# The first S5 output one projection unit later, and the squares of two norms added up on GpSimd

## What is computed

```
proj = h @ w_in + b_in
u_s5, cq, ckv, k_pe, u_sgu, v_sgu, gate_logits = split(proj)

# S5: a diagonal complex state-space model, 32 groups of 16 channels and 64 states
h_re, h_im = scan(a, bu)                 # along the tokens
y = h_re @ c_re - h_im @ c_im + d * u    # then gelu and a gate

# MLA: the two low-rank parts are normed before they are projected up
def rms_norm(x, g):
    return x * rsqrt(mean(x * x) + 1e-6) * g
q  = rms_norm(cq, q_norm)  @ w_q_up      # cq has 384 columns
kv = rms_norm(ckv, kv_norm) @ w_kv_up    # ckv has 256 columns
```

## Time and profile before

| what | value |
|---|---|
| median of three runs | 2423.53 us |
| profiled execution | 2425.12 us |
| its span on the core | 2423.30 us |
| TensorE busy | 2374.9 us, 98% |
| VectorE busy | 1390.1 us, 57% |
| GpSimd busy | 1673.5 us, 69% |
| ScalarE busy | 499.8 us, 21% |
| mean granted TensorE clock | 0.991 |

### The profile page before, as it was taken

How to read it: one execution, slowest core, us unless ns; L and a number is a source line. 1 busy time by engine, 2 the same in 40 slices (tenths; PEclk the granted TensorE clock), 3 DMA queues, 4 the chain that set the end, 5 groups by cost and what they waited for, 6 DMA issues and landing times.

```text
span 2423.3 us, 33639 instructions
## 1 busy us (share of the span) xinstructions
PE 2374.9 (98%) x11893; PEld 1952.5 (81%) x11893; DVE 1390.1 (57%) x1808; ACT 499.8 (21%) x957; POOL 1673.5 (69%) x757
## 2 busy tenths in 40 slices
PE   7999999999999999999999999999999999999998
PEld 5787777878888887888888878888878778888886
DVE  7987333475373477544555465534588577553547
ACT  5434221013000004211112230000132462000000
POOL 5435655777777777666666667777777557777775
PEclk8999999999999999999999999999999999999999
DMA  7222344322322322222222223322323112232331
GB/s 276 68 70 92 130 181 183 109 95 71 109 90 95 111 81 83 84 83 87 91 82 89 85 72 97 114 82 95 110 85 96 56 42 79 96 115 77 100 109 59
DMA packets 61729, 237.87 MB, mean 98 GB/s; under 512 B 7152, under 2 KB 12280, under 8 KB 58048
## 3 DMA queue, kind: packets, MB, share of 16 engines
q1 hardware_dynamic: 55152, 232.09, 28.4%
q10 hardware_dynamic: 6480, 4.51, 0.7%
HBM read 232.37 MB, written 2.10 MB: 97 GB/s over the span
## 4 chain that ended last, share of the span: by engine, by line
PE 85%; DVE 7%; DVEq 2%; ACT 1%; POOL 1%; DMA 1%; POOLq 1%; issue 1%; ACTq 1%
PE gg L696 19%; PE gg L697 19%; PE gg L698 19%; PE babcd L751 3%; PE babcd L752 3%; PE babcd L753 3%; PE gg L1124 2%; PE gg L1125 2%; PE gg L1126 2%; PE babcd L696 1%; PE babcd L698 1%; PE babcd L697 1%; DVE h_lo L2237 1%; DVE tb L2227 1%; DVEq L2228 1%
## 5 line engine op out<-in xcount | busy, mean ns | idle before, releaser
L696 PE MATMUL gg<-h_hi,w_hi 128*128 128x512 f32 x1512 | 595.9, 394 | 0.0
L698 PE MATMUL gg<-h_hi,w_lo 128*128 128x512 f32 x1512 | 589.7, 390 | 0.0
L697 PE MATMUL gg<-h_lo,w_hi 128*128 128x512 f32 x1512 | 589.6, 390 | 0.0
L516 POOL TENSOR_TENSOR w_hi<-raw,zero 128x1024 fp32r<-128x1024 f32 x192 | 378.0, 1969 | 295.9 <-PE gg L698 194.9
L518 POOL TENSOR_TENSOR w_lo<-raw,w_hi 128x1024 fp32r<-128x1024 f32 x192 | 479.8, 2499 | 28.0 <-issue 1.3
L507 POOL TENSOR_TENSOR w_hi<-raw,zero 128x1024 fp32r<-128x1024 f32 (+3 forms) x115 | 260.8, 2267 | 191.6 <-PE babcd L698 82.2
L509 POOL TENSOR_TENSOR w_lo<-raw,w_hi 128x1024 fp32r<-128x1024 f32 (+3 forms) x115 | 339.4, 2951 | 16.4
L696 PEld LDWEIGHTS gg<-h_hi,w_hi 128*128 128x128 f32 x1512 | 284.7, 188 | 63.5 <-issue 3.0
L698 PEld LDWEIGHTS gg<-h_hi,w_lo 128*128 128x128 f32 x1512 | 284.4, 188 | 59.8
L697 PEld LDWEIGHTS gg<-h_lo,w_hi 128*128 128x128 f32 x1512 | 284.5, 188 | 58.8 <-issue 0.3
L2328 DVE TENSOR_TENSOR ta<-ff_s,gg 128x512 f32<-128x512 f32 x63 | 43.3, 687 | 313.8 <-PE gg L698 313.8
(11 more groups left out here) (727 smaller groups left out, 3934.5 us busy)
## 6 DMA issues: line engine op xcount, KB each, us to landing
raw<-in_w_ff_in_a SPq DMA_DIRECT2D x66, 512.0 KB, 3.5
raw<-in_w_ff_in_b SPq DMA_DIRECT2D x66, 512.0 KB, 3.5
raw<-in_w_att_qk SPq DMA_DIRECT2D x48, 512.0 KB, 3.5
raw<-in_w_ff_out_a SPq DMA_DIRECT2D x24, 704.0 KB, 4.0
raw<-in_w_ff_out_b SPq DMA_DIRECT2D x24, 704.0 KB, 4.0
late_raw<-in_w_ada SPq DMA_DIRECT2D x16, 1024.0 KB, 4.9
raw<-in_w_ml SPq DMA_DIRECT2D x25, 512.0 KB, 3.5
raw<-in_w_merge_a SPq DMA_DIRECT2D x16, 768.0 KB, 5.1
```

The lines of the kernel that those rows point to most:

```text
L516: pool.tensor_tensor(hi, a, zero[:].to_broadcast([P, size * P]), ALU.add)
L696: pe.matmul(dst, w_hi[slot][:, blk], xs[0][:, k, :], start=k == 0, stop=False)
L697: pe.matmul(dst, w_hi[slot][:, blk], xs[1][:, k, :], start=False, stop=False)
L698: mm = pe.matmul(dst, w_lo[slot][:, blk], xs[0][:, k, :], start=False, stop=k == kb - 1)
```

## The change

- The sums of squares. GpSimd adds the square of unit 5, then of unit 6, onto the one of unit 4 in `sq[0]`, and the square of unit 8 onto the one of unit 7. TensorE then sums `sq[0]` once per norm: behind unit 7 for cq (it stood behind units 6 and 7), behind unit 13 for ckv. Three of five sums go, and VectorE has nothing to add up. `c_summed` now counts in order: first add, second add, sum of cq, third add, sum of ckv. ScalarE's waits for a free buffer follow that count.
- The adds stand in GpSimd's program behind the low parts of units 7, 8 and 10.
- The first S5 output stands behind unit 8 and not 7. The others stay behind 10, 13 and 15.
- VectorE reads the first output (`s5_y(0)`) behind `s5_batch(1)` and not before it.
- The waits for `s5_kb` in front of the first sums go.

```diff
 (GpSimd)
+            def add_squares(k):
+                pool.wait_ge(S["c_square"], k + 1)
+                pool.tensor_tensor(sq[0][:], sq[0][:], sq[1][:], ALU.add)
+                pool.drain().then_inc(S["c_summed"], 1)
             for u in range(2, 18):
                 low_part(u)
+                if u in (7, 8, 10):
+                    add_squares({7: 1, 8: 2, 10: 4}[u])
...
 (TensorE)
-            def low_rank_sum(k):
-                pe.wait_ge(S["c_square"], k + 1)
+            def low_rank_sum(n):
+                pe.wait_ge(S["c_summed"], (2, 4)[n])
                 for b in range(TB):
-                    at_col = k * TB + b
-                    mm = pe.matmul(bf[:, at_col:at_col + 1], sq[k % 2][:, b * P:(b + 1) * P], ones[:, 0:1], start=True, stop=True)
+                    at_col = n * TB + b
+                    mm = pe.matmul(bf[:, at_col:at_col + 1], sq[0][:, b * P:(b + 1) * P], ones[:, 0:1], start=True, stop=True)
                 mm.then_inc(S["c_summed"], 1)
...
-                if u == 6:
-                    pe.wait_ge(S["s5_kb"], 1)
-                    low_rank_sum(0)
-                    low_rank_sum(1)
                 if u in (6, 9, 12):
                     s5_inputs(u // 3 - 1)
-                if u in (7, 10, 13, 15):
-                    s5_outputs((u - 7) // 3 if u < 15 else 3)
+                if u in (8, 10, 13, 15):
+                    s5_outputs((8, 10, 13, 15).index(u))
                 if u == 7:
-                    low_rank_sum(2)
+                    low_rank_sum(0)
                 if u == 11:
                     low_rank_rows(0)
                 if u == 13:
                     pe.wait_ge(S["c_scaled"], 1)
-                    low_rank_sum(3)
-                    low_rank_sum(4)
+                    low_rank_sum(1)
...
 (ScalarE)
-                wait(act, "c_summed", k - 1)
-                act.activation(sq[k % 2][:], g[u % 2], ACT.Square, bias=proj_bias(u))\
+                wait(act, "c_summed", (0, 0, 1, 3, 2)[k])
+                act.activation(sq[(0, 1, 1, 0, 1)[k]][:], g[u % 2], ACT.Square, bias=proj_bias(u))\
...
 (VectorE)
-                part = [bf[:, k * TB:(k + 1) * TB] for k in range(5)]
-                tt(colv[:], part[3 * n], one_col[:, 0:TB], ALU.mult)
-                for k in ((1, 2), (4,))[n]:
-                    tt(colv[:], part[k], colv[:], ALU.add)
+                tt(colv[:], bf[:, n * TB:(n + 1) * TB], one_col[:, 0:TB], ALU.mult)
...
             angle(2)
-            s5_y(0)
             low_rank_total(0)
...
             s5_batch(1)
+            s5_y(0)
             low_rank_inverse(0)
```

## The result

The changed kernel took 2427.75 us (median of 10 runs, 2424.23 to 2430.90) against 2424.04 us for the kernel before (10 runs, 2423.40 to 2425.05): ratio 1.0018, 95% interval 1.0010 to 1.0025. It is slower by 3.7 us, inside the 0.2% that the prediction called no change, and 1.9 us above the time forecast (as a difference: +3.7, forecast +2.4). Its runs are spread over 6.7 us, those of the kernel before over 1.7 here (and over some 6 in the 30 to 33 runs that each later group made of it).

What follows compares the result with a forecast made beforehand. TensorE, busy 98% of the span, was taken as the bound. -9.0 (sums, stall, clock) +1.7 (first wait) +1.7 (inputs) +6.3 (second wait) +1.7 (clock) = +2.4 us, so 2425.9 us; range 2418.3 to 2428.7.

Steps and rivals of the forecast that it cites:

- the clock behind the first wait: TensorE's clock after the 1.7 us wait before the first sum: no cost taken, bound 1.7 us.
- What goes: TensorE in S5: three sums, the 3.06 us stall and 3.2 us of low clock go, 9.0 us in all.
- First new wait: TensorE before the first sum waits for GpSimd's two adds: 1.3 to 2.1 us, taken as 1.7.
- VectorE held by the additions: First S5 tile ends near 98.5, not 95.9; angle meets unit 10's low part (+2.1); second tile starts at about 106.
- Inputs: TensorE waits 1.7 us before the inputs of tile 2, for the second tile's PSUM reads on VectorE.
- Second output: TensorE waits 6.3 us for VectorE's late read, going on at 122.4 against 120.77; bounds 117.9 and 123.5.
- Clock behind the second wait: Lowered TensorE clock after the 6.3 us wait: costs from 0 to 3.2 us, taken as 1.7.
- After that: Units 11 to 15 follow as before, second sum saves 0.9: +0.7 us before the clock; no further waits.
- Rival 1: VectorE passes sines and angle before unit 10's low part; second output starts at 117.9: -3.8, 2419.7 us; chance 0.22.
- Rival 2: Waits come as forecast but TensorE's clock stays up: +0.7, 2424.2 us; chance 0.17.
- Rival 3: GpSimd does not hold VectorE as counted; TensorE pays only a 1.3 us wait: -7.7, 2415.8 us; chance 0.08.
- Rival 4: Both waits lower TensorE's clock, once the first passes about 2 us: +5.6, 2429.1 us; chance 0.11.

Runs made afterwards that it cites:

- e2: The kernel before with only the first S5 output moved behind unit 8 and its read behind the second S5 tile; 2419.70 us, ratio 0.9987.
- e8: The changed kernel with six small instructions put back in VectorE's stream at the end of its S5 stage; 2426.28 us, ratio 1.0011.
- e10: e2 with the second S5 output also one unit later, behind unit 11; all five sums on TensorE; 2420.30 us, ratio 0.9982.
- e3: The changed kernel with first output and read back where they were, so only additions and sums are new; 2429.34 us, ratio 1.0023.
- e9: e4 with twelve one-column matmuls on constants put where the kernel before has its three other sums; 2422.03 us, ratio 0.9996.
- e4: The changed kernel with GpSimd's three adds cut from 512 columns to 16, leaving out most of the sum of squares; 2426.91 us, ratio 1.0010.
- e1: The changed kernel with VectorE's read of the first S5 output put back before the second S5 tile; 2426.86 us, ratio 1.0012.
- e11: The changed kernel with the second S5 output behind unit 11 instead of unit 10; 2424.35 us, ratio 0.9999.
- e5: The changed kernel with TensorE's first sum moved behind unit 8's projection; 2426.26 us, ratio 1.0009.
- e12: The changed kernel with the edits of e5, e8 and e11 together; 2426.17 us, ratio 1.0010.

## Why the prediction was right and where it wasn't

The time (2427.75) lies in the range, and slower by less than 0.2% was the forecast. That the number came out near is partly luck. The +2.4 was forecast for the S5 stage and nothing behind it; in the profiled execution the stage gained 0.4 instead, and 1.9 us were lost at 427 us, which no step had. The waits and the engines behind them were named rightly; the clock behind the first wait, and with it the second wait's length, was not. All times in this part are on the scale of before.

- *What goes.* It went: the moved output has no stall, and 3.06 and the low clock behind it are gone. e2, which has only this part of the change, is 4.1 us faster than the kernel before.
- *First new wait.* 1.29, where I took 1.7 from bounds of 1.3 to 2.1. The addition itself took 1.29 and 1.38 (1.75 in the third), so the lower bound was right; the sum started at 90.48 against 90.7.
- *VectorE held by the additions.* The first tile ended at 98.03 (forecast 98.5), the angle met unit 10's low part (at 99.98, and at 98.39 in e8; forecast 98.5; it took 2.70, forecast 2.1 more than 0.69, measured 2.0), the second tile started at 104.99 (106).
- *Inputs.* The wait of 1.7 was 1.13 in e8's course and nothing in the changed kernel's profile.
- *Second output.* Forecast 122.4 after 6.3 of idling, because units 11 and 12 both fall into the second tile. e8's course is this one: 6.10 us, start at 121.83, stage +2.8 where the sum said +2.4. In the profiled execution and its repetition unit 12's low part missed the tile's last operation by 0.06 and 0.05 us, the read of `be` came at 118.19 where "about 121" was the sign of being right, the wait was 3.37 and the stage -0.4. The step that failed is the clock behind the first wait. I took nothing for it, with a bound of 1.7; it fell there in both profiles, cost 1.6, and I hadn't seen that a TensorE slowed by 1.6 would let VectorE end its tile before unit 12's low part.
- *Clock behind the second wait.* Taken 1.7; L964 took 4.09 against 2.32, so 1.8 in one course, 2.28 and a little more in the other.
- *After that.* "I carry a shift of TensorE at 150 us to the end of the span unchanged" was wrong. 1.9 us were lost at 427 (a shift of -2.75 on ScalarE's instructions at 403 us became -0.89 at 445), in every kernel with the six instructions fewer, and in none with them. With the stage's -0.4 that makes some +1.5 of the +3.7; the other 2 us stay open. e8's course in half of the runs would be enough, but no profile of the changed kernel shows it.

Rival 1 (2419.7) named the right mechanism, a low clock in unit 8 that lets VectorE get past a low part, at another place: the margin of under 1 us was at unit 12, not 10. Rival 2 (clock stays up) did not come. Rival 3 (GpSimd does not hold VectorE) is refuted by every row of 2.4 to 2.9. The Trainium skill (SBUF — State Buffer, SBUF: two separate sides) calls the port pair that VectorE and GpSimd share an exclusive lock that the loser waits out for the whole instruction, taken by VectorE's operations with two SBUF inputs or in a two-port mode; the trace agrees, also for TENSOR_SCALAR with its one input: 2.40 against 0.43 on 128x512, and 3.25 on 128x8. Rival 4 (both waits lower the clock, 2429.1) came true in its mechanism, though after a first wait of 1.29 and not of "about 2", and its sum was wrong: both did, and the low clock at 90.4 was taken out of the second wait instead of being added to it. Here terms that precede a wait on another engine couldn't be summed with it.

## What to carry to other kernels

Where two engines hold each other up and one of them follows TensorE, making TensorE faster can move the other's work under the slow engine; count what falls into each tile for both courses, and don't add up savings that come ahead of the same wait. Prefer the edit that moves the demand (the output and its read, -4.1 us here) to the one that takes work off an engine that was not waiting for it (the sums, -2.7 us of matmuls, for a loss). The first is shown by e2 and e10, the second by e3 and, for its mechanism, by e9 against e4. And take more than one profile before explaining 3 us: here the same instructions took a stage of 103.88 and one of 107.14 us.

## What the runs showed of the hardware

- The same idle time (1.29 or 1.30 us) before the same one-column sum was followed by a lowered clock in three profiles (the changed kernel's two and e1's; 0.56 in the window shown) and by 1.00 in two (e8, e11). The Trainium skill (TensorE: Matmul & The Clock Gate, What's actually happening) says that the gate's look at the engine runs free of the kernel's start; by that the two courses are expected, and the trace agrees.
- The length of the idle time alone did not decide it either. Before the 64 state matmuls of the first output TensorE sat idle for 3.47 us in both e5 and e12; behind it the clock was 1.00 in e5 (100.4 to 103.8) and 0.50 in e12 (100.2 to 103.4).
- VectorE pauses for 0.41 to 0.49 us at fixed places of its stream. Counted in the trace's records of the engine, drains and waits included, they lie at numbers 191 and 831 in the kernel before and the changed one, whichever instruction stands there, and in the changed one also at 319 and 959 (in e8 at 319, not at 959). Why there, no run shows. Removing six instructions at 100 and 150 us moved the pause of number 831 in front of an operation that lost a race for the shared ports by 0.28 us.
- GpSimd's addition of two 128x512 f32 tiles takes 1.28 to 1.75 us; on 16 columns it takes 0.22 to 0.67.
